# First two output-projection units: raw weights loaded and rounded during attention

## The reference

```python
# layer 0 (even)                                   # o_a: 512 wide, o_g: 4 heads x 128
o_g = block_attention(q_g, keys, vals, HD_B ** -0.5).reshape(B, L, HALF_W)
return jnp.concatenate([o_a, o_g], axis=-1) @ w_out, new_state
# layer 1 (odd)
o_d = block_attention(qf, keys, vals, (NOPE_D + ROPE_D) ** -0.5).reshape(B, L, HALF_W)
return jnp.concatenate([y_hy, o_d], axis=-1) @ w_out, new_state
# around both
xs = xs + ms[2] * os_                              # gated residual add of the projection
xs = xs + ms[5] * swiglu(modulate(xs, ms[3], ms[4]), w_ffn_in[i], w_ffn_out[i])
```

## Time and profile before

| | us |
|---|---|
| median of 3 runs | 1841.88 |
| range of the runs | 1839.98 to 1844.64 |
| profiled execution | 1844.08 |
| its span in the profile | 1842.3 |
| TensorE matmul busy | 1727.3 (94%) |
| VectorE busy | 846.9 (46%) |
| ScalarE busy | 578.7 (31%) |
| mean granted TensorE clock | 0.972 |

### The profile page before, as it was taken

One profiled execution on the slowest core, in us unless ns is written; L12 is line 12 of the kernel. 1 busy time (PEld: TensorE's weight loads), 2 busy tenths in 40 slices (PEclk: granted clock), 3 DMA queues, 4 the chain that ended last, 5 costly groups with the idle time before them and its releaser, 6 DMA issues.

```text
span 1842.3 us, 28588 instructions
## 1 busy us (share of the span) xinstructions
PE 1727.3 (94%) x11636; PEld 1592.2 (86%) x11636; DVE 846.9 (46%) x1499; ACT 578.7 (31%) x891; POOL 92.7 (5%) x68
## 2 busy tenths in 40 slices
PE   4899996797999999999999999898899999999997
PEld 2489985576999999999999897576899999999997
DVE  4624238574633433333337345854544433433344
ACT  3432454253432212211225344233342211211223
POOL 0000037000000000000001202000000000000002
PEclk9899998898999999999999999999999999999998
DMA  9245304003434253425325213000342133214212
GB/s 297 88 130 183 109 31 151 6 1 104 140 101 137 81 149 94 135 80 149 115 77 168 70 47 94 1 1 3 89 115 69 46 93 91 57 56 113 58 36 83
DMA packets 235895, 167.91 MB, mean 91 GB/s; under 512 B 7388, under 2 KB 231858, under 8 KB 235411
## 3 DMA queue, kind: packets, MB, share of 16 engines
q1 hardware_dynamic: 234992, 165.76, 30.2%
q10 hardware_dynamic: 802, 0.73, 0.2%
HBM read 160.61 MB, written 5.87 MB: 90 GB/s over the span
## 4 chain that ended last, share of the span: by engine, by line
PE 87%; DVE 7%; ACT 3%; issue 1%; DMA 1%; POOL 1%; ACTq 1%; DVEq 0%; SPq 0%; POOLq 0%
PE ua L891 12%; PE ub L891 12%; PE ua L893 12%; PE ua L892 12%; PE ub L892 12%; PE ub L893 12%; PE pm L821 2%; PE ua L1104 2%; PE ub L1104 1%; PE pt L1127 1%; PE pm L1127 1%; PE ua L1115 1%; PE ua L807 1%; DVE sct L2057 1%; DMA negt<-in_c_negt 0%
## 5 line engine op out<-in xcount | busy, mean ns | idle before, releaser
L1645 ACT ACTIVATE whi<-raw 128x1024 fp32r<-128x1024 f32 (+2 forms) x110 | 152.7, 1388 | 691.9 <-PE ub L893 342.0
L1924 DVE TENSOR_TENSOR wlo<-raw,whi 128x2048 fp32r<-128x2048 f32 (+2 forms) x127 | 219.9, 1732 | 60.3 <-ACT whi L1645 29.7
L891 PE MATMUL ub<-in_b_high,whi 128*128 128x386 f32 (+1 forms) x720 | 226.7, 315 | 11.3 <-DVE wlo L1924 7.4
L891 PE MATMUL ua<-in_a_high,whi 128*128 128x384 f32 (+1 forms) x736 | 230.1, 313 | 2.3 <-DVE in_a_rest L1965 1.9
L893 PE MATMUL ua<-in_a_high,wlo 128*128 128x384 f32 (+1 forms) x736 | 228.3, 310 | 0.0
L892 PE MATMUL ua<-in_a_rest,whi 128*128 128x384 f32 (+1 forms) x736 | 227.9, 310 | 0.0
L891 PE MATMUL ua<-in_b_high,whi 128*128 128x386 f32 (+1 forms) x720 | 225.5, 313 | 0.0
L891 PE MATMUL ub<-in_a_high,whi 128*128 128x256 f32 (+2 forms) x688 | 216.5, 315 | 8.9 <-DVE wlo L1924 8.9
L893 PE MATMUL ub<-in_b_high,wlo 128*128 128x386 f32 (+1 forms) x720 | 224.4, 312 | 0.0
L892 PE MATMUL ub<-in_b_rest,whi 128*128 128x386 f32 (+1 forms) x720 | 224.0, 311 | 0.0
L893 PE MATMUL ua<-in_b_high,wlo 128*128 128x386 f32 (+1 forms) x720 | 223.5, 310 | 0.0
(11 more groups left out here) (561 smaller groups left out, 2722.5 us busy)
## 6 DMA issues: line engine op xcount, KB each, us to landing
raw<-in_w_ffn_in SPq DMA_DIRECT2D x88, 512.0 KB, 5.1
modw<-in_w_mod SPq DMA_DIRECT2D x38, 1024.0 KB, 5.6
raw<-in_w_ffn_out SPq DMA_DIRECT2D x32, 512.0 KB, 3.9
raw<-in_w_in_even SPq DMA_DIRECT2D x10, 1024.0 KB, 7.6
raw<-in_w_in_odd SPq DMA_DIRECT2D x7, 1024.0 KB, 5.5
raw<-in_w_ffn_out SPq DMA_DIRECT2D x16, 384.0 KB, 3.3
mod_first<-in_w_mod SPq DMA_DIRECT2D x5, 1024.0 KB, 13.4
mod_tail<-in_w_mod SPq DMA_DIRECT2D x4, 1024.0 KB, 4.9
```

The lines of the kernel that those rows point to most:

```text
L891: pe.matmul(dst, wh, xh, start=first, stop=False)
L1645: act.activation(whi[s][:, 0:width], raw[s][:, 0:width], ACT.Copy).then_inc(w_hi, 1)
L1924: dve.tensor_tensor(wlo[s][:, 0:width], raw[s][:, 0:width], whi[s][:, 0:width].bitcast(F32), ALU.subtract).then_inc(w_lo, 1)
```

## The change

Two new places hold the raw weights of each projection's first two units: `raw_out[0]` is the upper half of whi0, `raw_out[1]` the upper half of raw1 (both unused by units of this size). SyncE loads them in layer 0 when the last logarithm ahead of attention is made (`o_ln`), in layer 1 when the last inverse transform is multiplied (`y_mm`), and no longer after attention. ScalarE rounds them into the lower half of whi inside its attention loop, after loop steps 8 and 10. VectorE takes the remainders where it did before, after its attention loop, but reads raw_out. The loads after attention start with the two modulation loads (layer 0) or the third unit (layer 1). The waits of ScalarE are the same in kind: the load's counter and `unit_done`. TensorE's and GpSimd's programs are not changed.

```diff
+        raw_out = [sb("raw_out0", [P, 1024], at=sb_at["whi0"] + 4096), sb("raw_out1", [P, 1024], at=sb_at["raw1"] + 4096)]
...
-            def out_loads(u0, w, kt, with_mod=False):
+            def first_out_loads(u0, w):
+
+                for u in (u0, u0 + 1):
+                    src = w[:, (u - u0) * P:(u - u0 + 1) * P].rearrange("(k p) n -> p k n", p=P)
+                    sp.dma_start(raw_out[u % 2][:, :].rearrange("p (k n) -> p k n", k=KD), src).then_inc(w_raw[u % 2], 16)
+
+            def out_loads(u0, w, kt, with_mod=False, first=True):
                 def body(i, last):
-                    for j in range(2):
+                    for j in range(2 if first or not isinstance(i, int) or i else 0):
                         src = w[:, bass.ds(i * 256 + j * P, P)].rearrange("(k p) n -> p k n", p=P)
                         ring_load(u0 + 2 * i + j, 0, (u0 + j) % 2, src, kt, P)
...
-                pairs(sp, KD, body, peel_first=with_mod)
+                pairs(sp, KD, body, peel_first=with_mod or not first)
...
+            sp.wait_ge(o_ln, TT)
+            first_out_loads(U_OUT0, i_["w_out_even"][0])
             sp.wait_ge(at_lo, 20)
-            out_loads(U_OUT0, i_["w_out_even"][0], KD, with_mod=True)
+            out_loads(U_OUT0, i_["w_out_even"][0], KD, with_mod=True, first=False)
...
+            sp.wait_ge(y_mm, 4)
+            first_out_loads(U_OUT1, i_["w_out_odd"][0])
             sp.wait_ge(at_lo, 40)
-            out_loads(U_OUT1, i_["w_out_odd"][0], KD)
+            out_loads(U_OUT1, i_["w_out_odd"][0], KD, first=False)
...
-            def attention(layer, scale, dst_hi):
+            def out_high(u):
+                act.wait_ge(w_raw[u % 2], 16 * (u // 2) + 16)
+                act.wait_ge(unit_done, u - 1)
+                act.activation(whi[u % 2][:, 0:1024], raw_out[u % 2][:, :], ACT.Copy).then_inc(w_hi, 1)
+
+            def attention(layer, scale, dst_hi, u_out):
...
+                    if n in (8, 10):
+                        out_high(u_out + (n - 8) // 2)
...
-            for u in (U_OUT0, U_OUT0 + 1):
-                ring_high(u, u // 2, u % 2, 1024)
...
-            for u in (U_OUT1, U_OUT1 + 1):
-                ring_high(u, u // 2, u % 2, 1024)
...
-            def w_rest(u, s, width):
+            def w_rest(u, s, width, src=raw):
                 dve.wait_ge(w_hi, u + 1)
-                dve.tensor_tensor(wlo[s][:, 0:width], raw[s][:, 0:width], whi[s][:, 0:width].bitcast(F32),
+                dve.tensor_tensor(wlo[s][:, 0:width], src[s][:, 0:width], whi[s][:, 0:width].bitcast(F32),
                                   ALU.subtract).then_inc(w_lo, 1)
...
             for u in (U_OUT0, U_OUT0 + 1):
-                w_rest(u, u % 2, 1024)
+                w_rest(u, u % 2, 1024, raw_out)
...
             for u in (U_OUT1, U_OUT1 + 1):
-                w_rest(u, u % 2, 1024)
+                w_rest(u, u % 2, 1024, raw_out)
```

More of the change, by code:

```diff
@@ L1637, in attention @@
                                        ).then_inc(at_hi, 1)
-            attention(0, HD ** -0.5, hhi)
+                    if n in (8, 10):
+                        out_high(u_out + (n - 8) // 2)
+            attention(0, HD ** -0.5, hhi, U_OUT0)
             def ring_high(u, hf, s, width, up=None):
@@ L1826, in _ @@
                 act.activation(hhi_b[:, c, :], tmp[:, c % 2], ACT.Copy).then_inc(y_hi, 1)
-            attention(1, (NOPE + ROPE) ** -0.5, hhi_b)
-            for u in (U_OUT1, U_OUT1 + 1):
-                ring_high(u, u // 2, u % 2, 1024)
+            attention(1, (NOPE + ROPE) ** -0.5, hhi_b, U_OUT1)
             out_stage(U_OUT1, 1024, (2048, NF // 2 + 1), 3, hin_a[0])
```

## The result

| | before, us | after, us |
|---|---|---|
| median | 1842.95 (4 runs, 1839.98 to 1844.64) | 1831.56 (4 runs, 1830.97 to 1834.05) |
| profiled execution | 1844.08 | 1831.89 |
| its span | 1842.3 | 1830.1 |
| mean granted clock | 0.972 | 0.978 |

The ratio of after to before is 0.9941 (95% interval 0.9929 to 0.9953): 0.6% faster. Forecast were 1831.4 us, 0.57% faster, range 1825.0 to 1838.5.

The account below looks back on a forecast made before the run. TensorE, busy 94% of the span, was taken to bound the kernel, so only its standstill at the two seams could be gained: 1841.88 less 5.0 and 5.5, other terms 0, gives 1831.4 us, range 1825.0 to 1838.5.

Parts of the forecast that it names:

- Part 1: At both attention-to-projection seams load and rounding leave the chain; wlo starts 437.65 to 437.73 at the first; gains 5.02 and 5.47 us.
- Part 2: TensorE's low clock around each seam still costs 2.3 us, returning 4 to 5 us after the first matmul: effect 0.
- the bounds: Clock effect over both seams: from 4.6 us gained if never low to 4.4 us lost if low twice as long.
- signs of being wrong: First unit other than 9.4 us, TensorE waiting some 0.5 us on ScalarE, or third-unit load over 14 us after first matmul.
- rival A: At each seam the clock stays high or returns at once: another 2.3 us gained, 1826.8 us in all; chance 0.12.
- Part 3: Two added ScalarE roundings of 1.06 us inside each attention stay hidden: cost 0, or 4.2 us without any cover.
- Part 4: SyncE's early loads hold up nothing in its queue; the third unit's load behind attention has 4 us cover: cost 0.
- The sum: Over both seams -5.0 - 5.5 + 0 + 0 = -10.5 us, all on TensorE's path, giving a median of 1831.4 us.

Follow-up runs that it names:

- the two with fillers: Fp32 products nobody reads added to TensorE in attention's last jobs: on the changed kernel 1827.45 us, on the kernel before 1844.37 us.
- three roundings: Changed kernel with two more 128x1024 ScalarE roundings ahead of each of the four in attention: 1836.93 us.
- early remainder: Changed kernel with the first unit's wlo in its own place, made by VectorE inside attention after loop step 12: 1831.98 us.
- waits by parts: Changed kernel with first-unit wlo made inside attention, and TensorE waiting for attention's remainders by the part of the sum reading them: 1829.40 us.
- control set: Runs on one chip with the changed kernel repeated unaltered as yardstick: 1831.57 us against 1843.24 for the kernel before, ratio 0.9937.

## Why the prediction was right

**Part 1, the seams: right.** Predicted were 5.0 and 5.5 us, measured 5.08 and 5.54. VectorE's wlo started 0.09 us ahead of the end of the last remainder, at the early end of what I had allowed. The dear link was the load (4.3 and 4.8 us); the rounding brought 0.75.

**Part 2, the clock: its size was off.** I took the cost of the low level as unchanged. It grew by 0.5 and 0.75 us per seam in the first pair of profiles and by 1.2 and 1.0 in the second, since the clock came back 5.8 us after the first matmul and not 4 to 5. The first matmul moved ahead by more than the moment of return did: in the first pair the low stretch shrank from some 13.6 us to 10.2 at both seams, the gap by 5.1 and 5.5. Behind gaps of 1.8 us, with the thin end as it was, the first unit took 9.4 to 9.8 us in all seven cases, behind gaps of 6.9 to 7.5 us 8.55 to 9.24 in all five. The added cost lay inside the bounds, but a first unit other than 9.4 us was one of my own signs of being wrong: measured in the same way, to ScalarE's next rounding, it took 9.98 us. That the fall belongs to the thin end and not to the gap, on which I rested the refusal of rival A, was shown by the kernel without any gap and by the two with fillers.

The high clock is worth 2.6 us per seam (9.78 less 7.18), and TensorE had it at the seam only where the thin end was filled and the gap short. The Trainium skill ("TensorE: Matmul & The Clock Gate", Part 1: The HAM clock gate) has it that idleness lowers the clock, that activity releases it, and that the count of slow matmuls differs from run to run. The two profiles of the kernel before agree (first units of 9.24 and 8.55 us at the first seam), and so does the fall in the 6.92 us of gap behind filled work; the fall in the thin end shows that no long idle time is needed, since TensorE never stood still there for over 0.93 us in any profile.

**Part 3, ScalarE in attention: right.** The delay was 0.94 us and no wait arose. The margin ahead of TensorE, 1.6 us less the rounding by the prediction, was confirmed by the waits behind three roundings. In the first attention (375 to 420) VectorE waited for TensorE 9.6 + 1.5 us, before 9.7 + 1.3, and for nothing else.

**Part 4, SyncE: right, with a thin margin.** In the changed kernel little was left to load behind 448 (14 GB/s in 448 to 452), and ScalarE waited for TensorE and not for the third unit's load, which had landed 0.9 us before ScalarE took it up at 448.31:

```profile
448.31 1.06 ACT L1663 ACTIVATE whi<-raw 128x1024 fp32r<-128x1024 f32 x1 [11.48 <-PE ub L904]
```

In the kernels with the early remainder or with fillers the load is late for ScalarE: 11.8 us of its idle time ahead of the third unit's whi ended with the DMA, in the kernel with waits by parts. TensorE still had cover, since the second unit ran; it waited for no third unit in any of them.

**The sum: right in size, in part by luck.** The seams bring 10.6 us, the first units take back 1.3 to 2.2, which leaves some 9. The medians differ by 11.4, 11.7 us in the control set. The other 2 us come from the stretch between the seams, which the change doesn't touch behind its first unit. In the nine profiles without fillers that rest took 831.8 us in the four in which the clock was low for 3.4 us between 456 and 1264 (the changed kernel twice, the change in layer 0, the early remainder), and 833.6 to 835.0 (0.4 of it ScalarE's waits of the three roundings) in the five in which it was low for 10.1 or 10.2 us (the kernel before twice, loads alone early, three roundings, waits by parts). The 6.7 us more at 1.2 GHz are worth up to 3.4, so the clock can account for the difference. Both profiles of the kernel before are of the slower kind and both of the changed kernel of the quicker, but so few profiles leave open whether the earlier start makes the kinder places likelier or whether this was chance. The median itself was met to 0.2 us (1831.56 for 1831.4) since a second error stood against the larger gain: the three runs that I started from had a median 1.1 us below that of all four. The lower bound of the range is 1824.9 by its own terms and not 1825.0, which changes nothing.

## What to carry to other kernels

At the seam between two stages, read the chain from the last result to the first matmul link by link, and move first the link that costs most and needs nothing of the stage ahead: here a load of 3.9 us whose place was free. Work moved into another engine's loop is free up to the time by which that engine's next result is early, which may have to be read two operations further on (here it lay within 0.1 us of the engine's idle time, so that these runs don't show which of the two is the limit); beyond it, it costs one to one. Below a few us, compare waits and stretches cut at the same events, not medians, and take a second profile of the kernel before: the clock moved untouched stretches by 2 to 3 us between profiles.

## What the runs showed of the hardware

The granted clock fell to 1.2 GHz at 434.0, in attention's thin end, in the kernel whose seam has no gap at all (waits by parts of the sum), and stayed at 2.4 GHz where the thin end was filled (1.00 in 432 to 438). Behind filled work it came through a gap of 1.82 us (the changed kernel with fillers) and fell inside one of 6.92 us, at 438.7 (the kernel before with fillers). A shorter gap alone gave back part of its gain: first units of 9.4 to 9.8 us behind 1.8 us, of 8.55 to 9.24 behind some 7. Products that nobody reads made the changed kernel 4.1 us faster (1831.57 to 1827.45).
